# Seven-product weight stages: high weights against both halves of x in one 512-column matmul, results formed from PSUM partial sums

## What is computed

```python
# second layer, hn is [512, 2048], three gate matrices of [2048, 2048] each
hn = rms_norm_2(x, norm_gain)
gate_logits = (hn @ w_in)[..., -3 * D_MODEL:]
g = sigmoid(gate_logits.reshape(b, s, 3, D_MODEL))
y = g[:, :, 0] * ua + g[:, :, 1] * ub + g[:, :, 2] * uc
return x + y @ w_out          # w_out is [2048, 2048]
```

## Time and profile before

| | before |
|---|---|
| time, median of 3 runs | 2146.0 us (2145.42 to 2148.44) |
| span of the profiled execution | 2144.3 us |
| PE busy | 2114.5 us, 99% |
| VectorE busy | 1638.5 us, 76% |
| ScalarE busy | 920.1 us, 43% |
| chain that ended last | PE 83%, DVE 6%, ACT 3%, DVEq 3%, DMA 2% |
| L1172 to L1174, 256 columns | 3 times 1568 matmuls |
| L425 to L427, 512 columns | 3 times 2000 matmuls |

### The profile page before, as it was taken

How to read it: one execution, slowest core, us unless ns; L and a number is a source line. 1 busy time by engine, 2 the same in 40 slices (tenths; PEclk the granted TensorE clock), 3 DMA queues, 4 the chain that set the end, 5 groups by cost and what they waited for, 6 DMA issues and landing times.

```text
span 2144.3 us, 35680 instructions
## 1 busy us (share of the span) xinstructions
PE 2114.5 (99%) x12168; PEld 1835.5 (86%) x12168; DVE 1638.5 (76%) x2684; ACT 920.1 (43%) x1581; POOL 76.9 (4%) x145
## 2 busy tenths in 40 slices
PE   7899999999999999999999999999999999999999
PEld 6788888788887999999998888888787888888999
DVE  6887877775667888888886666666868776777887
ACT  6434454433335444444444444444545444223433
POOL 0000000000000000000000000000000000010000
PEclk9999999999999999999999999999999999999999
DMA  9766432565544343343333222222222223665543
GB/s 381 266 243 234 178 96 97 208 219 191 177 144 132 123 144 128 121 142 131 119 105 119 89 88 88 88 90 87 70 81 78 89 89 121 205 213 181 193 142 109
DMA packets 85935, 310.76 MB, mean 145 GB/s; under 512 B 9765, under 2 KB 12213, under 8 KB 77505
## 3 DMA queue, kind: packets, MB, share of 16 engines
q1 hardware_dynamic: 71568, 258.24, 35.6%
q0 software_dynamic: 11520, 46.68, 6.2%
q10 hardware_dynamic: 2738, 4.47, 0.6%
HBM read 284.41 MB, written 24.94 MB: 144 GB/s over the span
## 4 chain that ended last, share of the span: by engine, by line
PE 83%; DVE 6%; ACT 3%; DVEq 3%; DMA 2%; issue 1%; ACTq 0%
PE bank L425 18%; PE bank L427 18%; PE bank L426 18%; PE bank L1172 9%; PE bank L1174 9%; PE bank L1173 9%; DVE w_lo L419 2%; ACT w_hi L409 1%; PE bank L554 1%; PE bank L585 1%; DMA w_raw<-stream 1%; DMA front_raw<-stream 1%; PE bank L567 1%; DVEq L414 1%; ACT probs L637 1%
## 5 line engine op out<-in xcount | busy, mean ns | idle before, releaser
L425 PE MATMUL bank<-x_hi,w_hi 128*128 128x512 f32 x2000 | 789.1, 395 | 3.6 <-ACTq L1357 1.2
L427 PE MATMUL bank<-x_hi,w_lo 128*128 128x512 f32 x2000 | 779.1, 390 | 0.0
L426 PE MATMUL bank<-x_lo,w_hi 128*128 128x512 f32 x2000 | 778.6, 389 | 0.0
L419 DVE TENSOR_TENSOR w_lo<-w_raw,w_hi 128x512 fp32r<-128x512 f32 x468 | 324.2, 693 | 315.6 <-ACT w_hi L409 286.6
L409 ACT ACTIVATE w_hi<-w_raw 128x512 fp32r<-128x512 f32 x468 | 295.9, 632 | 572.4 <-PE bank L427 477.0
L425 PEld LDWEIGHTS bank<-x_hi,w_hi 128*128 128x128 f32 x2000 | 375.4, 188 | 94.4 <-issue 8.9
L1172 PE MATMUL bank<-x_hi,pw_hi 128*128 128x256 f32 x1568 | 444.0, 283 | 0.8 <-issue 0.7
L1173 PE MATMUL bank<-x_lo,pw_hi 128*128 128x256 f32 x1568 | 443.7, 283 | 0.0
L1174 PE MATMUL bank<-x_hi,pw_lo 128*128 128x256 f32 x1568 | 443.7, 283 | 0.0
L427 PEld LDWEIGHTS bank<-x_hi,w_lo 128*128 128x128 f32 x2000 | 375.4, 188 | 79.6
L426 PEld LDWEIGHTS bank<-x_lo,w_hi 128*128 128x128 f32 x2000 | 375.7, 188 | 75.4 <-issue 0.2
(11 more groups left out here) (214 smaller groups left out, 1840.5 us busy)
## 6 DMA issues: line engine op xcount, KB each, us to landing
w_raw<-stream SPq DMA_DIRECT2D x234, 512.0 KB, 3.7
pw_raw<-stream SPq DMA_DIRECT2D x112, 512.0 KB, 4.6
wmod<-w_mod_rows SPq DMA_DIRECT2D x32, 1024.0 KB, 6.7
front_raw<-stream SPq DMA_DIRECT2D x16, 1024.0 KB, 9.0
wmod<-w_mod_rows POOLq DMA_DIRECT2D x16, 1024.0 KB, 5.2
sig_store<-logits POOLq DMA_DIRECT2D x45, 256.0 KB, 2.5
sig_back<-sig_store SPq DMA_DIRECT2D x8, 768.0 KB, 5.9
gate_sig<-sig_store SPq DMA_DIRECT2D x7, 768.0 KB, 5.8
```

The costliest lines, as they stand in the source:

```text
L419: nc.vector.tensor_tensor(w_lo[:, q, :], raw_quarter(s), w_hi[:, q, :].bitcast(F32), ALU.subtract).then_inc(lo_ready, 1)
L425: nc.tensor.matmul(bank_ap[:, :tokens], hi, x_hi[:, kx, :], start=start, stop=False)
L426: nc.tensor.matmul(bank_ap[:, :tokens], hi, x_lo[:, kx, :], start=False, stop=False)
L427: return nc.tensor.matmul(bank_ap[:, :tokens], lo, x_hi[:, kx, :], start=False, stop=stop)
```

## The change

The high and low parts of x become two planes of one tensor (`x1`, `x2`). A product is then 8 times two matmuls instead of 8 times three: the high weights against 256 high and 256 low columns of x in one matmul of 512 columns that fills a whole bank, and the low weights against the high x, 256 columns, into the first half of the bank. A product's value is the sum of the two halves of its bank. Products 0, 3 and 5 add up in one bank (`in_both`), 2 and 4 in another (`in_column`), 1 and 6 have their own (`in_row`, `in_second`). ScalarE copies four whole banks a pair at certain moments (`first_term`, `column_term`, `sum_terms` twice). VectorE forms the four blocks of the result with both halves side by side (`c11`, `c12`, `c22`, `c21`, 512 wide) in `row_parts`, then each row by adding the halves (`row_of`), then the multiplication as before, or the residual (`add_back`). The four weight sums stay on VectorE; signs are turned so that all are additions. The six rotating raw buffers become four fixed ones, one for each block, and two buffers are used by `row_parts`.

```diff
+        x1 = sb("x1", [P, 2, KT, T], F32R, at_x1)
+        x2 = sb("x2", [P, 2, KT, T], F32R, at_x2)
+        x1_hi, x1_lo, x2_hi, x2_lo = x1[:, 0], x1[:, 1], x2[:, 0], x2[:, 1]
...
-        pw_raw = [sb(f"pw_raw{n}", [P, 8 * P], F32, at_x3 + 4 * KB * n) for n in range(6)]
-        w_sum = [sb(f"w_sum{n}", [P, 8 * P], F32, at_x3 + 4 * KB * n) for n in (6, 7)]
+        a21, a22, a11, a12, first_sum, later_sum = [
+            sb(name, [P, 8 * P], F32, at_x3 + 4 * KB * n)
+            for n, name in enumerate(("a21", "a22", "a11", "a12", "first_sum", "later_sum"))]
+        row_parts = [sb(f"row_parts{n}", [P, 2, 2, HALF], F32, at_x3 + 4 * KB * (6 + n)) for n in range(2)]
...
+            return (a11, a12, first_sum, later_sum, later_sum, first_sum, a22)[f.o]
...
+            def buffer_free(pair, slot, sem, count):
...
+                if first_of_section(pair):
+                    sp.wait_ge(t_ready, pair.c // PAIRS * KT // 2 + slot + 1)
                 else:
...
-                load_factor(l)
+                    sp.wait_ge(sem, count.value())
...
+            def load_a22(pair):
+                src = factor_part(pair, 3)
+                buffer_free(pair, 1, pw_lo_ready, pair.times(7))
+                sp.dma_start(a22[:, :], src).then_inc(a22_loaded, 16)
...
+            def load_a12(pair):
+                src = factor_part(pair, 1)
+                buffer_free(pair, 3, w_sum_made, pair.times(4) - 1)
+                sp.dma_start(a12[:, :], src).then_inc(a12_loaded, 16)
+
+            def load_pair(pair):
+                load_a12(pair)
+                load_a21(pair)
+                load_a11(pair)
+                load_a22(pair)
+            load_pair(At(0))
+            for n in (1, 2):
...
+                to, x, odd, tokens, adds = [
+                    (in_both[f.j], x1, 0, lower, False), (in_row, x1, 1, lower, False),
+                    (in_column, x2, 0, upper, False), (in_both[f.j], x2, 1, upper, True),
+                    (in_column, x1, 1, upper, True), (in_both[f.j], x2, 0, lower, True),
+                    (in_second, x2, 1, lower, False)][f.o]
...
+                if f.o in (3, 4, 5):
+                    pe.wait_ge(term_copied, (pair.times(4) + (f.o - 2)).value())
...
-                    nc.tensor.matmul(to, hi, x_hi[:, 2 * k + odd, tokens], start=k == 0, stop=False)
-                    nc.tensor.matmul(to, hi, x_lo[:, 2 * k + odd, tokens], start=False, stop=False)
-                    mm = nc.tensor.matmul(to, lo, x_hi[:, 2 * k + odd, tokens], start=False, stop=k == 7)
+                    nc.tensor.matmul(to[:, :].rearrange("p (a t) -> p a t", a=2), hi, x[:, :, 2 * k + odd, tokens],
+                                     start=k == 0 and not adds, stop=False, skip_group_check=adds)
+                    mm = nc.tensor.matmul(to[:, :HALF], lo, x[:, 0, 2 * k + odd, tokens], start=False, stop=k == 7,
+                                          skip_group_check=adds)
...
+                        act.wait_ge(c11_made, f.pair.value())
+                    nc.scalar.activation(first_term[:, :], in_both[f.j][:, :], ACT.Copy).then_inc(term_copied, 1)
+                if f.o == 3:
+                    act.wait_ge(product_done, (f.pair.times(7) + 3).value())
+                    if f.pair.positive():
+                        act.wait_ge(c22_made, f.pair.value())
+                    nc.scalar.activation(column_term[:, :], in_column[:, :], ACT.Copy).then_inc(term_copied, 1)
+                if f.o == 4:
+                    act.wait_ge(product_done, (f.pair.times(7) + 4).value())
+                    if f.pair.positive():
+                        act.wait_ge(c21_made, f.pair.value())
+                    nc.scalar.activation(sum_terms[:, :], in_both[f.j][:, :], ACT.Copy).then_inc(term_copied, 1)
+                if f.o == 6:
+                    act.wait_ge(product_done, (f.pair.times(7) + 6).value())
+                    act.wait_ge(c12_made, (f.pair + 1).value())
+                    nc.scalar.activation(sum_terms[:, :], in_both[f.j][:, :], ACT.Copy).then_inc(term_copied, 1)
...
+                if f is None:
...
+                to, one, two, landed = {2: (first_sum, a21, a22, a22_loaded), 3: (later_sum, first_sum, a11, a11_loaded),
+                                        4: (later_sum, later_sum, a12, a12_loaded), 5: (first_sum, a11, a21, a21_loaded)}[f.o]
                 dve.drain()
                 if f.o == 2:
...
+                    dve.wait_ge(a21_loaded, (f.pair + 1).times(16).value())
+                dve.wait_ge(landed, (f.pair + 1).times(16).value())
+                nc.vector.tensor_tensor(to[:, :], one[:, :], two[:, :], ALU.add).then_inc(w_sum_made, 1)
...
+            def c11(f):
+
+                dve.drain()
+                dve.wait_ge(product_done, (f.pair.times(7) + 2).value())
+                dve.wait_ge(term_copied, (f.pair.times(4) + 1).value())
+                nc.vector.tensor_tensor(row_parts[0][:, 0], two_parts(first_term), two_parts(in_row), ALU.add).then_inc(c11_made, 1)
...
+            def c12(f):
+
+                dve.drain()
+                dve.wait_ge(product_done, (f.pair.times(7) + 5).value())
+                dve.wait_ge(term_copied, (f.pair.times(4) + 3).value())
+                nc.vector.tensor_tensor(row_parts[0][:, 1], two_parts(sum_terms), two_parts(in_column), ALU.add).then_inc(c12_made, 1)
...
+            def c22(pair):
+
+                dve.drain()
+                dve.wait_ge(term_copied, (pair + 1).times(4).value())
+                nc.vector.scalar_tensor_tensor(row_parts[1][:, 1], two_parts(sum_terms), -1.0, two_parts(column_term),
+                                               ALU.mult, ALU.subtract).then_inc(c22_made, 1)
...
+            def c21(pair):
+
+                dve.drain()
+                dve.wait_ge(product_done, (pair + 1).times(7).value())
+                nc.vector.tensor_tensor(row_parts[1][:, 0], two_parts(in_second), two_parts(sum_terms), ALU.subtract).then_inc(c21_made, 1)
...
+            def row_of(to, slot):
+
+                nc.vector.tensor_tensor(two_parts(to), row_parts[slot][:, :, 0], row_parts[slot][:, :, 1], ALU.add)
...
+            def first_row(pair):
+                dve.drain()
+                dve.wait_ge(sig_stored[0], (pair + 2).times(16).value())
+                row_of(logits[0], 0)
...
+            def second_row(pair):
+                dve.drain()
+                dve.wait_ge(sig_stored[1], (pair + 1).times(16).value())
+                row_of(logits[1], 1)
...
             def dve_product(l, i=None):
...
-                if f.o in (0, 1, 2, 6) and f.ahead(3):
...
+                if f.o in (0, 2, 6):
                     weight_sum(f.ahead(3))
...
+                if f.o == 1 and not f.pair.positive():
+                    plain_gate(2)
+                if f.o == 2:
+                    if follows:
+                        c22(before)
+                    c11(f)
+                if f.o == 3 and follows:
+                    c21(before)
+                    if l >= PRODUCTS:
+                        result_row(result_of + 1, 1)
                     else:
...
-                elif f.o == 3 and f.pair.positive():
-                    second_row(f.pair - 1, (f.j - 1) % 3)
...
-                if f.o == 4:
-                    dve.wait_ge(product_done, (f.pair.times(7) + 4).value())
-                    dve.wait_ge(term_copied, (f.pair + 1).value())
-                    nc.vector.tensor_tensor(later_terms[:, :], pair_sum[:, :HALF], terms[:, HALF:], ALU.add).then_inc(second_made, 1)
-                    dve.drain()
-                    nc.vector.tensor_tensor(pair_sum[:, HALF:], later_terms[:, :], row_2[f.j][:, HALF:], ALU.add).then_inc(fourth_made, 1)
...
-                    first_row(f.pair)
+                        second_row(before)
...
+                if f.o == 4 and follows:
+                    if l >= PRODUCTS:
+                        add_back(result_of + 1)
+                    else:
+                        logits_of(1)
+                if f.o == 5:
+                    c12(f)
+                    if l >= PRODUCTS:
+                        result_row(result_of + 2, 0)
+                    else:
+                        first_row(f.pair)
                 if f.o == 6:
-                    dve.drain()
-                    dve.wait_ge(product_done, (f.pair.times(7) + 6).value())
-                    nc.vector.tensor_tensor(later_terms[:, :], later_terms[:, :], third[:, :HALF], ALU.add).then_inc(third_made, 1)
+                    if l >= PRODUCTS:
+                        add_back(result_of + 2)
+                    else:
+                        logits_of(0)
                 factor_lo(f.ahead(2))
...
+                if f.o == 1:
+                    weight_sum(f.ahead(3))
...
+            def result_row(n, slot):
+
+                dve.drain()
+                dve.wait_ge(result_stored[n % 2], 16 * (n // 2) + ONE)
+                row_of(result[:, n % 2], slot)
+
+            def add_back(n):
 
```

(76 more changed lines are left out.)

218 lines of the change are left out of this document (98 added, 120 removed).

## The result

The changed kernel takes 2218.7 us in the median (2216.48 to 2219.89) against 2146.6 for the kernel before on the same chip: a ratio of 1.0334 (95% interval 1.0319 to 1.0348). The forecast was 2204, the range 2170 to 2232. Its profiled execution has a span of 2216.3 us, 72.0 more than before, where the sum had said 58.

The account below looks back on a forecast made before the run. VectorE was to replace TensorE as the bound in the pairs: +45.7 us in the gates, +11.8 in w_out, +0.25 in the tail, together +58 on the profiled 2144.3, a 2202 span and 2204 us median; range 2170 to 2232.

Parts of the forecast that it names:

- part 2: VectorE's work per pair: 19.03 us against 17.49; its pace 21.9 in the loop, 20.95 written out, above TensorE's 19.42.
- Part 1: TensorE's matmuls: a product goes from 2.88 to 2.77 us, a pair from 20.16 to 19.42, hidden if VectorE is the bound.
- Two terms in the loop: VectorE's loop pair: 17 register waits with gaps of 0.16 us, and a stall of 0.8 us for a22's landing.
- TensorE's idle places: In a loop pair TensorE idles 1.7 us ahead of product 4 and 0.4 to 0.5 ahead of 5 and 1.
- The other three blocks have 5 us or more and cost nothing: Loads of the weight blocks other than a22 land before they are needed, at no cost.
- The stall in `w_out`: In w_out, a22's load queues behind x_back's: VectorE stalls 1.3 us a pair; the section grows by 11.8 us.
- The tail: After the last product, two additions of 256 instead of one of 512: +0.25 us.
- A: Rival: VectorE bound, but a22's load lands in time or nearly, taking off up to 24 us: 2180; chance 0.18.
- B: Rival: TensorE stays the bound and the change gains what its matmul count promises: 2125 us; chance 0.05.
- C: Rival: VectorE bound and idling TensorE loses its full clock, a product taking 5.5 us, in half the pairs: 2430; chance 0.02.
- D: Rival: a22 landings of 4.6 us and more, or gaps of 0.2 with two waits: 2224 to 2234 us; chance 0.11.
- The Trainium skill's rule on semaphores: VectorE waits cost nothing beyond the drain: loop pair 20.7 us, time some 18 us under the forecast.

Follow-up runs that it names:

- run 5: Changed kernel with the edits of run 1 and run 4, a11 loaded first at the start of w_out, a22 loaded ahead of x_back: 2175.4 us, ratio 1.0133.
- run 2: Kernel before, with three unused additions of 512 columns a pair added to VectorE's queue: 2195.8 us, ratio 1.0225.
- run 3: Kernel of run 1 with three of the four weight sums of each pair left out: 2134.9 us, ratio 0.9947.
- run 1: Changed kernel with the next pair's first weight sum (a21 + a22) made two steps later on VectorE: 2187.9 us, ratio 1.0189.
- run 7: Changed kernel with only two load-order edits: a11 first at the start of w_out, a22 ahead of x_back in w_out: 2209.5 us, ratio 1.0289.
- run 4: Changed kernel with VectorE's loop over 15 pairs written out, so its waits have constant values: 2211.6 us, ratio 1.0294.
- run 6: Kernel of run 5 with one of the four weight sums (a11 + a21, for product 5) made on GpSimd instead of VectorE: 2198.3 us, ratio 1.0239.

## Why the prediction came out as it did

**The bound (part 2) was right.** VectorE's work was 19.00 for 19.03, c22 with its two arithmetic steps 0.69 where 0.72 was taken, and run 5 gives the pace without stalls as 20.94 for 20.95. That it is the cause, and not only busy, is shown from both sides: its work alone costs 49 us in the kernel before (run 2), and three sums less bring the changed kernel under the one before (run 3).

**Part 1 was right and worth nothing.** 19.45 for 19.42 us of TensorE a pair, in run 3. The 0.7 us that it saves a pair never reaches the end of the pair while VectorE needs 21 to 22.

**Two terms in the loop were off and met, which is luck.** I gave 17 instructions a gap of 0.16. In the pair of after eleven of them have 0.15 to 0.18 and one is the wait for a22; the other five, the sums for products 3, 4 and 5, c21 and the second row, start 0.08 to 0.10 after the instruction ahead, though each waits on a register value (the sums at 864.43 and 865.75 are 1.32 apart, 1.23 of it work). That is 0.35 us less than the forecast. And the wait for a22 is on average 1.22 us idle in the 15 pairs of the loop, thus some 1.06 beyond the usual gap, where I had 0.8; its landing took 4.1 us in the median for my 3.8. Together the loop's pairs take 340.9 us for 340.5. The +48.2 for +45.7 in the gates comes for the larger part from the written-out pairs behind the loop: they wait 1.62 and 1.93 for a22, and two of them take 45.2 us for 43.7. Run 1 takes the wait for a22 away and 0.86 us a pair with it.

**TensorE's idle places: both there, in other sizes.** Ahead of product 4 1.10 instead of 1.7, ahead of product 1 1.05 instead of 0.4 to 0.5, ahead of 5 hardly any. TensorE's busy share in the pair is 90% and not 86%, as the modelled ends of its matmuls reach into the waits. The total hangs on VectorE's period and not on these.

**"The other three blocks have 5 us or more and cost nothing" failed.** It was read in the running pair and is true there. At the start of `w_out` there is no pair before it: SyncE sends a12, a21, a11, a22 in the running order, while product 0 wants a11. Before, the block that product 0 needs was the first of six to leave, 13 us ahead of the product (1998.44):

```profile
1985.43 11.28 SPq L991 DMA_DIRECT2D pw_raw<-stream  x6
```

After, a11 is third, leaves 2.8 us after its buffer is free and lands 7.2 us after its issue. That is the 4.06 us of wait, and run 7, which changes only the order of loads, has it no more. I put 0 to +1 for everything between the sections; it is +4.9.

**The stall in `w_out` was mis-sized.** 1.3 was taken for a22 behind x_back; the waits are 1.34, 2.39, 2.29, 1.98, 2.48 and 2.94 us, 13.4 in all, and the section came out at +17.4 for +11.8 (counted as the forecast counts, from the weight sum for product 3, +16.7; the rest of it is part of the late start). With a22 ahead they are 0.84 to 1.44 (run 7). The place was right, its price was under by 0.8 a pair: the load of x_back in front costs about 1 us, not 0.4.

**The tail was mis-sized too.** +1.5 for +0.25. I counted what stands behind the last product when all else is done. But VectorE begins the last pair's c22 only at 2210.45, after a wait of 0.38 for a store of an earlier result, and six additions of 256 follow it, past the last matmul at 2211.3:

```profile
2210.45 0.69 DVE L2048 SCALAR_TENSOR_TENSOR row_parts<-sum_terms,column_term 128x512 f32<-128x512 f32 x1 [0.38 <-DMA result_features<-result]
...
2211.24 0.42 DVE L2325 TENSOR_TENSOR result<-row_parts 128x256 f32<-128x256 f32 x1
...
2213.40 0.42 DVE L2334 TENSOR_TENSOR result<-result,bank 128x256 f32<-128x256 f32 x1
```

Together the four terms make the 14 us between forecast and result: 2.5 in the gates, 4.9 between, 5.6 in `w_out`, 1.2 in the tail. All four lie on the same side; that the forecast holds is the work of VectorE's pace, which is 28 pairs of the sum.

**The rivals.** A (a22 in time, 2180) did not happen, but run 1 takes the wait away: 2187.9. The price is the same mechanism; of the 8 us left the start of `w_out` is 4, and the late high part, 0.13 us over the usual gap in most pairs, some 2.5. B (TensorE bound, 2125) needs three of VectorE's sums gone: 2134.9. C (the clock falls) did not cost the time: the granted clock is full in the pairs of the gates, and where it fell, in `w_out`, VectorE still set the pace (last section). D (landings at 4.6 and more for the sigmoid's store) did not happen in the gates, where a22's landings took 4.1 in the median; in `w_out` they took 5.1, but for x_back's load in front (run 7), not for a sigmoid.

**The Trainium skill's rule on semaphores** ("VectorE: DVE Perf Modes", section "The DRAIN you can't avoid": a semaphore costs nothing extra), cited in part 2, holds here for one wait on a constant value: run 4 gives 0.09 with one wait and 0.16 with two. In the loop, with waits on a register, it is 0.15 to 0.18 in eleven places and 0.08 to 0.10 in five; why these five differ no run shows. By the rule the loop pair would be 20.7 before stalls; with the stall of 1.0 that is 21.7 and not 22.60.

## What to carry to other kernels

An engine that is busy 76 to 87% of a stretch can be at its pace already: add the start-to-start distances of its instructions, not their durations, and compare with the other engine's period before you give it work. When rotating buffers become one buffer for each block, follow the load from the instruction that frees it to the first reader, past everything in its queue, and do that once for the running pair and once for the first one, where the order of loads may be wrong for the first product. And a saving on TensorE is worth only what the engine behind it leaves over.

## What was new about the hardware

GpSimd's addition of 128x1024 takes 2.41 us (2.38 to 2.77 in 28) and stops a VectorE operation with two SBUF sources until it is done: 3.40 us instead of 1.23. So an idle GpSimd was no spare adder beside a VectorE that was the bound. Whether a VectorE operation that reads a bank of PSUM would be stopped too, run 6 does not show: in all 28 pairs one operation with two SBUF sources stood beside GpSimd's sum and took 2.78 to 3.48 us, in 27 the low part of product 3, in one a weight sum.

In `w_out` TensorE lost its full clock behind three of its six longest waits. Here the matmuls behind the 2.16 us wait of the pair 2096.74 to 2119.79, the other waits of over 1.7 us between pairs, and windows of the changed kernel (granted clock: third figure from the end):

```profile
2100.12 0.73 PE L1195 MATMUL bank<-x,pw_hi 128*128 128x512 f32 x1 [2.16 <-DVE pw_lo L2012]
...
2102.15 0.63 PE L1195 MATMUL bank<-x,pw_hi 128*128 128x512 f32 x1
...
2102.79 0.63 PE L1195 MATMUL bank<-x,pw_hi 128*128 128x512 f32 x1
...
2104.23 0.40 PE L1195 MATMUL bank<-x,pw_hi 128*128 128x512 f32 x1
...
2104.58 0.39 PE L1195 MATMUL bank<-x,pw_hi 128*128 128x512 f32 x1
...
2123.17 0.50 PE L1195 MATMUL bank<-x,pw_hi 128*128 128x512 f32 x1 [1.79 <-DVE pw_lo L2012]
...
2169.53 0.50 PE L1195 MATMUL bank<-x,pw_hi 128*128 128x512 f32 x1 [2.25 <-DVE pw_lo L2012]
...
2193.22 0.50 PE L1195 MATMUL bank<-x,pw_hi 128*128 128x512 f32 x1 [2.56 <-DVE pw_lo L2012]
```

```profile
2100.00:2103.00 3.00, 2.88 (x9) 2.50 (x10) 2.73 (x4) 1.54 (x2) 0.00 (x0) 0.54 0.55 167
...
2110.00:2115.00 5.00, 5.00 (x31) 4.38 (x30) 4.49 (x6) 2.60 (x3) 0.00 (x0) 1.00 0.50 146
...
2125.00:2127.00 2.00, 2.00 (x8) 1.71 (x7) 1.91 (x2) 1.01 (x2) 0.00 (x0) 0.50 0.01 3
2170.00:2173.00 3.00, 3.00 (x19) 2.62 (x18) 2.82 (x3) 1.54 (x2) 0.00 (x0) 1.00 0.36 138
2194.00:2197.00 3.00, 3.00 (x19) 2.62 (x18) 2.82 (x3) 1.55 (x2) 0.00 (x0) 1.00 0.35 135
```

A 512 and a 256 take 0.64 us together at the lower level (1.2 GHz) and 0.35 at full clock. This lasted from 2100.1 to 2103.4, some 1.5 us of lost TensorE time; behind the wait of 4.06 us the same (0.64 from 2052.4 to 2055.5), and again behind a wait of 1.79 us (0.50 of full clock in 2125 to 2127). The length of the wait does not decide it: behind waits of 2.25 and 2.56 us, and of 1.53, the clock stayed full (1.00). What does, these rows do not show. Behind the waits of up to 1.70 us in the gates it stayed full (1.00 over 700 to 1175). The lost time does not show in the end: the pair 2096.74 to 2119.79 takes 23.05 us, VectorE's 20.95 and its wait for a22. Rival C had the mechanism, in a few products of `w_out` instead of in half of the pairs; a product wholly at the lower level would take 8 x 0.64 = 5.1 us by these rows, where C took 5.5. Where TensorE sets the pace such a stretch could cost its 1.5 us on top of the wait; that is an estimate, and no run shows it.
